# Two directions of a triangular inversion share the array: left products of one beside right products of the other

## What is computed

```python
def _rwkv7_step(S, inp):
    r, w, k, v, kk, a = inp
    sa = jnp.einsum('dbhij,dbhj->dbhi', S, -kk)
    S = S * w[..., None, :] + sa[..., None] * (kk * a)[..., None, :] + v[..., None] * k[..., None, :]
    y = jnp.einsum('dbhij,dbhj->dbhi', S, r)
    return S, y
...
    S0 = jnp.zeros((N_DIR, B, H, N, N), f32)
    _, ys = lax.scan(_rwkv7_step, S0, seq)
    y = jnp.moveaxis(ys[:, 0] + jnp.flip(ys[:, 1], axis=0), 0, 1)
```

## Time and profile before

| | us |
|---|---|
| median of 3 runs | 2883.79 (2883.17 to 2884.23) |
| profiled execution, its own device time | 2885.75 |
| profiled execution, span of the trace | 2883.9 |
| PE busy | 2832.7 (98%) |
| DVE busy | 1456.6 (51%) |
| ACT busy | 1081.3 (37%) |
| first left product of iteration 0 to start of the next step | 2206.1 to 2234.3 |
| the same stretch of iterations 1, 2, 3 | 2250.5 to 2285.1, 2302.8 to 2341.0, 2355.2 to 2389.3 |

### The profile page before, as it was taken

One profiled execution on the slowest core, in us unless ns is written; L12 is line 12 of the kernel. 1 busy time (PEld: TensorE's weight loads), 2 busy tenths in 40 slices (PEclk: granted clock), 3 DMA queues, 4 the chain that ended last, 5 costly groups with the idle time before them and its releaser, 6 DMA issues.

```text
span 2883.9 us, 43564 instructions
## 1 busy us (share of the span) xinstructions
PE 2832.7 (98%) x19606; PEld 2337.1 (81%) x19606; DVE 1456.6 (51%) x1431; ACT 1081.3 (37%) x1176; POOL 146.1 (5%) x74
## 2 busy tenths in 40 slices
PE   9999999999999999999999999999999998999998
PEld 7788778888888888888888888788877886888886
DVE  6676553443455544443364444466657665543432
ACT  5554542222454832222342222442235532332222
POOL 1000010000110010000110000240000000100001
PEclk9999999999999999999999999999999999999999
DMA  4220022223222022233222223322231003222232
GB/s 150 74 77 2 31 88 102 97 93 110 103 100 88 35 73 94 97 102 110 102 88 102 95 95 115 104 83 81 88 125 35 4 6 135 101 96 97 102 102 74
DMA packets 44953, 249.09 MB, mean 86 GB/s; under 512 B 8507, under 2 KB 12347, under 8 KB 17248
## 3 DMA queue, kind: packets, MB, share of 16 engines
q1 hardware_dynamic: 43616, 242.11, 24.6%
q10 hardware_dynamic: 1152, 4.19, 0.4%
HBM read 237.90 MB, written 8.39 MB: 85 GB/s over the span
## 4 chain that ended last, share of the span: by engine, by line
PE 91%; DVE 5%; ACT 3%; issue 1%; DMA 0%; SPq 0%; DVEq 0%; ACTq 0%
PE ps L667 76%; PE ps L2919 4%; PE ps L1515 1%; PE ps L2501 1%; PE ps L2211 1%; PE ps L3979 1%; PE ps L2926 1%; PE ps L2485 1%; PE ps L3962 1%; PE ps L3991 1%; PE ps L2182 0%; DVE wlo L274 0%; PE ps L3097 0%; DVE gdn_conv L1147 0%; ACT whi L268 0%
## 5 line engine op out<-in xcount | busy, mean ns | idle before, releaser
L274 DVE TENSOR_TENSOR wlo<-wraw,whi 128x2048 fp32r<-128x2048 f32 x210 | 486.6, 2317 | 911.5 <-ACT whi L268 907.3
L268 ACT ACTIVATE whi<-wraw 128x2048 fp32r<-128x2048 f32 x210 | 402.1, 1915 | 900.0 <-PE ps L667 900.0
L667 PE MATMUL ps<-ffn_xh,whi 128*128 128x512 f32 x1408 | 549.2, 390 | 0.2 <-DVE wlo L274 0.2
L667 PE MATMUL ps<-ffn_xh,wlo 128*128 128x512 f32 x1408 | 547.8, 389 | 0.0
L667 PE MATMUL ps<-ffn_xl,whi 128*128 128x512 f32 x1408 | 547.8, 389 | 0.0
L667 PEld LDWEIGHTS ps<-ffn_xh,whi 128*128 128x128 f32 x1408 | 264.3, 188 | 56.9 <-DVE wlo L274 1.0
L667 PEld LDWEIGHTS ps<-ffn_xl,whi 128*128 128x128 f32 x1408 | 264.3, 188 | 55.6 <-issue 0.7
L667 PEld LDWEIGHTS ps<-ffn_xh,wlo 128*128 128x128 f32 x1408 | 264.3, 188 | 54.9
L667 PE MATMUL ps<-ffn_uh,whi 128*128 128x512 f32 x704 | 274.1, 389 | 0.0
L667 PE MATMUL ps<-ffn_uh,wlo 128*128 128x512 f32 x704 | 273.9, 389 | 0.0
L667 PE MATMUL ps<-ffn_ul,whi 128*128 128x512 f32 x704 | 273.9, 389 | 0.0
(11 more groups left out here) (524 smaller groups left out, 4446.5 us busy)
## 6 DMA issues: line engine op xcount, KB each, us to landing
wraw<-in_weights SPq DMA_DIRECT2D x211, 1024.0 KB, 4.8
gates_kept<-gates_tmp ACTq DMA_DIRECT2D x8, 512.0 KB, 4.0
mix_gate<-gates_kept SPq DMA_DIRECT2D x8, 512.0 KB, 11.0
h<-in_x SPq DMA_DIRECT2D x4, 512.0 KB, 9.0
mix_y<-hz_kept SPq DMA_DIRECT2D x2, 1024.0 KB, 6.3
out<-out SPq DMA_DIRECT2D x4, 512.0 KB, 3.1
wraw<-in_weights SPq DMA_DIRECT2D x2, 512.0 KB, 7.4
ple_raw<-in_p SPq DMA_DIRECT2D x4, 256.0 KB, 5.1
```

The costliest lines, as they stand in the source:

```text
L268: c.nc.scalar.activation(c.whi[:, j % 2, :], c.wraw[:, j % 2, :], ACT.Copy).then_inc(c.hi_ready, 1)
L274: c.nc.vector.tensor_tensor(c.wlo[:, j % 2, :], c.wraw[:, j % 2, :], c.whi[:, j % 2, :].bitcast(F32), ALU.subtract).then_inc(c.lo_ready, 1)
L667: last = nc.tensor.matmul(pair[:, m, :], a, b, start=opens and n == 0 and wa + xa == 0, stop=closes and n == len(ks) - 1 and wa == 1)
```

## The change

`pe_left` of one direction and `pe_right` of the other are emitted together, by `pe_phase`, in eleven phases at the odd slots 7, 9, ... 27 (`PHASES`). Phase m holds left product m (level m/2, direction m mod 2; phases 0 to 9) and right product m-1 (phases 1 to 10), chunk by chunk: two matmuls of the left, two of the right. The waits of both stand ahead of the phase, and both semaphores are raised at its end. The left product is written `across`, so its result lies on the other head's partitions; ACT moves it back with two ACTIVATEs of 64 partitions in place of one of 128. DVE's instructions are the same, at the phases' slots. The transposes of `K` and `B`, the steps, prepare and finish stay at their slots.

```diff
+PHASES = range(7, 28, 2)
...
-        elif 7 <= s < 26:
-            l, what = divmod(s - 7, 4)
-            if what < 2:
-                self.pe_left(pe, k, l, what)
-            else:
-                self.pe_right(pe, k, l, what - 2)
+        elif s in PHASES:
+            self.pe_phase(pe, k, (s - 7) // 2)
...
-        elif s == 27:
-            self.pe_right(pe, k, LEVELS - 1, 1)
...
+    def lefts(self, m):
+
+        return divmod(m, 2) if m < 2 * LEVELS else None
+
+    def rights(self, m):
+
+        return divmod(m - 1, 2) if m else None
+
+    def pe_phase(self, pe, k, m):
+        left, right = self.lefts(m), self.rights(m)
+        if left is not None:
+            self.left_ready(pe, k, *left)
+        if right is not None:
+            self.right_ready(pe, k, *right)
+        for n in range(NCH):
+            if left is not None:
+                last_left = self.pe_left(n, *left)
+            if right is not None:
+                last_right = self.pe_right(k, n, *right)
+        if left is not None:
+            last_left.then_inc(*self.done("Y"))
+        if right is not None:
+            last_right.then_inc(*self.done("Z"))
...
+    def pe_left(self, n, l, d):
+        out = self.bank(self.y_bank(d))
+        return self.across(lambda r: out[r, n, :], lambda r: self.LT[r, d, n, :], lambda r: self.X[r, d, n, :])
...
-        self.c.nc.scalar.activation(self.Y[:, d, :, :], self.bank(self.y_bank(d)), ACT.Copy).then_inc(*self.done("Yc"))
+        low, high = self.halves()
+        made = self.bank(self.y_bank(d))
+        self.c.nc.scalar.activation(self.Y[low, d, :, :], made[high], ACT.Copy)
+        self.c.nc.scalar.activation(self.Y[high, d, :, :], made[low], ACT.Copy).then_inc(*self.done("Yc"))
```

More of the change, by code:

```diff
@@ L3027, in pe_values, with left_ready @@
         last.then_inc(*self.done("MV"))
-    def pe_left(self, pe, k, l, d):
-        out = self.bank(self.y_bank(d))
-        if l == 0:
-            pe.wait_ge(*self.at("LT", 2 * k + d))
+    def lefts(self, m):
[17 more added lines that the diff above has]
+            last_right.then_inc(*self.done("Z"))
+    def left_ready(self, pe, k, l, d):
         if l:
@@ L3036, in pe_left @@
         else:
+            pe.wait_ge(*self.at("LT", 2 * k + d))
             pe.wait_ge(*self.at("Xi", 2 * k + d))
@@ L3042, in pe_left, with right_ready @@
                 pe.wait_ge(*self.at("Yc", 10 * k - 2))
-        for n in range(NCH):
-            last = self.both(lambda r: out[r, n, :], lambda r: self.LT[r, d, n, :], lambda r: self.X[r, d, n, :])
-        last.then_inc(*self.done("Y"))
-    def pe_right(self, pe, k, l, d):
-        bank, XT = self.z_bank(l, d), self.XT[k % 2]
+    def pe_left(self, n, l, d):
+        out = self.bank(self.y_bank(d))
+        return self.across(lambda r: out[r, n, :], lambda r: self.LT[r, d, n, :], lambda r: self.X[r, d, n, :])
+    def right_ready(self, pe, k, l, d):
         pe.wait_ge(*self.at("Yc", 10 * k + 2 * l + d))
@@ L3059, in pe_right @@
                 pe.wait_ge(*self.at("ys", k))
-        for n in range(NCH):
-            if l < LEVELS - 1:
-                last = self.both(lambda r: self.columns(self.halved(bank)[r, n, :], l),
-                                 lambda r: XT[r, d, n, :], lambda r: self.side(self.Y[r, d, n, :], l, d))
-            else:
-                last = self.both(lambda r: self.columns(self.halved(bank)[r, n, :], l), lambda r: self.Y[r, d, n, :],
-                                 lambda r: self.side(XT[r, d, n, :], l, 1 - d))
-        last.then_inc(*self.done("Z"))
+    def pe_right(self, k, n, l, d):
+        bank, XT = self.z_bank(l, d), self.XT[k % 2]
+        if l < LEVELS - 1:
+            return self.both(lambda r: self.columns(self.halved(bank)[r, n, :], l),
+                             lambda r: XT[r, d, n, :], lambda r: self.side(self.Y[r, d, n, :], l, d))
+        return self.both(lambda r: self.columns(self.halved(bank)[r, n, :], l), lambda r: self.Y[r, d, n, :],
+                         lambda r: self.side(XT[r, d, n, :], l, 1 - d))
     def pe_turn(self, pe, src, banks, name):
@@ L3180, in act_build @@
                     .then_inc(*self.done("ysc"))
-        if 7 <= s < 26 and (s - 7) % 4 < 2:
-            self.act_left(act, k, *divmod(s - 7, 4))
+        if s in PHASES and self.lefts((s - 7) // 2) is not None:
+            self.act_left(act, k, *self.lefts((s - 7) // 2))
         elif s in (26, 28):
@@ L3361, in dve_build @@
                 .then_inc(*self.done("ys"))
-        if 7 <= s < 26 and (s - 7) % 4 >= 2:
-            l, what = divmod(s - 7, 4)
-            self.dve_right(dve, k, l, what - 2)
-        elif s == 27:
-            self.dve_right(dve, k, LEVELS - 1, 1)
+        if s in PHASES and self.rights((s - 7) // 2) is not None:
+            self.dve_right(dve, k, *self.rights((s - 7) // 2))
         if s == SLOTS - 1:
```

## The result

The changed kernel takes 2898.81 us (median, 2895.58 to 2901.20); the kernel before took 2884.01 beside it. The ratio is 1.0048, with a 95% interval of 1.0035 to 1.0061: slower by about 14 us. The forecast was 2883.4, between 2877.5 and 2890. It was wrong.

What follows compares the result with a forecast made beforehand. PE's queue was taken to bound the four stretches, with a chain through ACT limiting the phases afterwards. The iterations' 2.55 - 1.4 - 2.5 - 0.65 = -2.0, plus 1.6 for stalls, gave -0.4: 2883.4 us, range 2877.5 to 2890.

Steps and rivals of the forecast that it cites:

- The bound: In the four level stretches PE's queue, busy 94 to 97%, sets the time, but little can go before another engine is late.
- rival A: In the four stretches PE was the bound, so its whole saving of 34 us comes off: 2850; chance 4%.
- The quarters: In each phase left and right products run together in the array: 64 records in 0.94 us.
- rival E: In the phases the quarters don't run together; nine phases take 0.94 us more, +30, 2914; chance 2%.
- The link, 2.30 us: From phase start to next phase start through ACT's two half copies: 1.15 + 1.09 + 0.06 us at least.
- the walk: Each queue followed in order through the four iterations' stretches: 2.55 - 1.4 - 2.5 - 0.65 = -2.0 us.
- surcharge: Groups starting after a stall on PE cost 0.05 us more, about eight more stalls per iteration: +1.6 us in all.
- Rival C: ACT's copy shifted between partitions is slower; halves that don't overlap, with 0.1 us between, give +8.4, 2891.8; chance 10%.
- Rival D: TensorE's clock falls in the gappier stretches; five episodes of 1.5 us work at twice the time, +7.5, 2890.9; chance 5%.
- Rows 9: Profile rows of iteration 4: granted clock 1.00 with PE busy 3.24 of 5 us, 0.79 at 3.26 of 5.

Runs made afterwards that it cites:

- k0_fill: Change in iteration 0 alone, with six pairs of small identity products behind seven phases, against the kernel before: 2891.83 us, ratio 1.0021.
- later_only: Change in iterations 1 to 3 alone, iteration 0 as in the kernel before: 2888.11 us beside 2885.93, ratio 1.0004.
- full_copy: Whole change with one copy of 128 partitions per Y, leaving its halves swapped (other numbers computed): 2884.59 us, ratio 0.9997 to the kernel before.
- k0_full: Change in iteration 0 alone with one copy of 128 partitions, halves of Y swapped, against the kernel before: 2887.21 us, ratio 1.0005.
- full_lean: Change with one copy of 128 partitions (halves swapped), older-copy wait dropped and last copy's wait put last: 2883.71 us beside 2885.93 before, ratio 0.9984.
- lean_fill: Change with older-copy wait dropped, last copy's wait last, six pairs of fillers in all four iterations: 2892.29 us, ratio 1.0022 to the kernel before.

## Why the prediction was wrong

**The bound.** Right: taking work from PE gives nothing by itself, a chain through ACT takes over, and rival A did not come. PE's busy time in the stretches fell by 17 us and its idle time rose by 30. That the busy time would fall to about 95 was wrong; it is 111.9.

**The quarters.** Right: the records of a phase start within 0.93 us (2222.33 to 2223.26), where 0.94 was forecast for 64, and rival E did not come.

**The link, 2.30 us.** This is the step that failed first. "What follows on ACT starts 0.49 after its start" was read from a pair of full copies and used for two halves, which start 0.61 apart. "0.06 is the time from DVE's end to PE's start" was read from a single wait and used for a row of four, where it is 0.25. With 0.04 for the start of the copy this makes 2.64, 0.34 more in each link. For nine or ten links in each of four iterations that is 12 to 14 us if every link were at its floor; where steps or the sigmoids set the pace it is hidden. Measured at full clock against the walk without its surcharge:

| iteration | walk | measured at full clock | from |
|---|---|---|---|
| 0 | +2.55 | +6.9 | `k0_fill` |
| 1 | -1.4 | +1.1 | `later_only` |
| 2 | -2.5 | -1.1 | `later_only` |
| 3 | -0.65 | +2.3 | `later_only` |
| sum | -2.0 | +9.2 | |

The walk runs from the first phase to the next step and the marks from copy to copy, so a row compares two slightly different spans. The order of the four, 0 the worst and 2 the best, was right, and so was that iteration 2 gains. The sum was off by 11.2, of which the surcharge for stalls had only 1.6. Rival C named the first term: it priced a link at 0.21 us more and came to +8.4. The copies alone were 0.11 worse than forecast, the row of waits, in no rival, 0.19.

**The clock.** Rival D was the mechanism and its size was too small, and its chance of 5% much too small. It was priced at 1.5 us for each of five episodes, from one row of work at 0.79. In the profile of the change the clock stays at 1.2 GHz for most of 2214 to 2242, and this costs 4.7 us in iteration 0 alone, by fillers whose own cost is already taken off. Rows 9 had shown both outcomes at the same busy share; that was a reason for an open chance, not for a small one. The two terms also feed each other: the gap of 1.49 us in which PE stands idle is what the longer link makes. With one copy the gap is 0.89, and in `full_copy` the clock fell only once in iteration 0, for a few us; but in `k0_full`, with the same phases, it fell twice, and in `full_lean` from 2222 to 2234. So the length of the gap alone does not settle when it falls.

**The open remainder.** Links at full clock (9.2) and the clock in iteration 0 (4.7) make 13.9 of the 14.8 us. The first number comes from single traces and the second from medians, so the match is closer than its parts are known; the marks of the change alone give 13.9 at the last one.

## To carry to other kernels

A chain link is priced from rows with the same shape of copy, the same first partition and the same row of waits; a gap or a lag borrowed from another pair of instructions was off by 0.1 and 0.2 us here, and ten links multiply it. Where an edit takes work from PE and leaves idle gaps between its bursts, the fall of the clock belongs in the main case and not among the rivals. Moving a result across partitions costs a second full copy: 14 us here, the difference between the change and `full_copy`, clock included.

## What the hardware showed beyond that

- Copies on ScalarE of 64 partitions take 0.59 us, like those of 128. In the rows shown they overlap a neighbour by 0.10 us only if both start at the same partition; otherwise they start 0.01 to 0.03 after its end.
- The lag from the end of the work to TensorE's start is 0.05 us with that wait first in its row, whatever stands behind it, 0.14 with it last of three, and 0.25 with it third of four.
- Twelve small products (six pairs) behind each of seven phases kept the granted clock at 1.00 in the profile of `k0_fill`, where it fell to 0.50 without them, and gave 4.7 us; with one copy they kept it too and gave nothing, and in `lean_fill` it fell in spite of them.
